# Points in the selection of experts weigh about 1.37 times as much when picks are handed out

## What is computed

```python
q = (xc @ w_q).reshape(t, PEER_HEADS, 2, PEER_QDIM // 2)
sc = jnp.einsum('thpc,hpnc->thpn', q, sub_keys)
v_half, i_half = lax.top_k(sc, PEER_TOPK_HALF)                 # 16 lists of 128 scores, 16 kept of each
cand = (v_half[:, :, 0, :, None] + v_half[:, :, 1, None, :]).reshape(t, PEER_HEADS, -1)
cand_idx = (i_half[:, :, 0, :, None] * PEER_NKEYS + i_half[:, :, 1, None, :]).reshape(t, PEER_HEADS, -1)
top_s, pos = lax.top_k(cand, PEER_TOPK)
expert = jnp.take_along_axis(cand_idx, pos, axis=-1)
g = jax.nn.softmax(top_s, axis=-1)
u = u_tab[expert]
act = jax.nn.gelu(jnp.einsum('thkd,td->thk', u, xc), approximate=False)
return jnp.einsum('thk,thkd->td', g * act, v_tab[expert])
```

## Time and profile before

| | us |
|---|---|
| median of 3 runs | 2128.93 |
| lowest and highest | 2127.93, 2129.14 |
| the profiled execution | 2127.96 |
| its span, first to last instruction | 2126.2 |
| affected feeds, first gathered row to third expert list | about 180 to 1286 |
| fourth feed, to its last row | to 1665 |

### The profile page before, as it was taken

How to read it: one execution, slowest core, us unless ns; L and a number is a source line. 1 busy time by engine, 2 the same in 40 slices (tenths; PEclk the granted TensorE clock), 3 DMA queues, 4 the chain that set the end, 5 groups by cost and what they waited for, 6 DMA issues and landing times.

```text
span 2126.2 us, 20672 instructions
## 1 busy us (share of the span) xinstructions
PE 1665.4 (78%) x6490; PEld 1005.3 (47%) x6490; DVE 1490.8 (70%) x3129; ACT 785.7 (37%) x2050; POOL 643.3 (30%) x524
## 2 busy tenths in 40 slices
PE   8797777667777865887778478765767899999998
PEld 4473343622323453333344433554333465668986
DVE  5378876897756688976666897668787465566654
ACT  1213452234424422432452235212555343454432
POOL 0013444335433343643344354425444000000000
PEclk9999989879898987989889799987888999999999
DMA  7358999999999999999999999999999785574452
GB/s 274 148 213 365 421 399 421 419 421 422 418 421 401 416 421 411 413 420 421 416 373 421 412 389 421 421 421 422 400 412 392 308 306 202 194 281 160 178 178 99
DMA packets 105803, 746.87 MB, mean 351 GB/s; under 512 B 12896, under 2 KB 13536, under 8 KB 16608
## 3 DMA queue, kind: packets, MB, share of 16 engines
q0 software_dynamic: 73728, 536.90, 61.4%
q1 hardware_dynamic: 31536, 207.08, 25.1%
q10 hardware_dynamic: 432, 1.57, 0.2%
HBM read 744.46 MB, written 1.05 MB: 351 GB/s over the span
## 4 chain that ended last, share of the span: by engine, by line
PE 39%; DMA 23%; DVE 20%; ACT 10%; issue 6%; DVEq 1%; PEldq 1%; PEld 0%; ACTq 0%; SPq 0%; POOL 0%; POOLq 0%
DMA sb_work<-in_peer_uv,sb_expert 17%; PE ps_acc L1570 11%; PE bank L496 5%; DVE sb_work L1534 5%; PE bank L1363 4%; DVE sb_x L1542 3%; DMA sb_ninth<-in_peer_uv,sb_expert 3%; PE bank L2060 2%; DMA sb_wring<-in_peer_w_q 2%; ACT L1550 2%; PE bank L777 2%; PE bank L566 2%; PE ps_acc L566 2%; PE ps_acc L568 2%; PE ps_acc L567 2%
## 5 line engine op out<-in xcount | busy, mean ns | idle before, releaser
L2694 POOL DMA_INDIRECT sb_work<-in_peer_uv,sb_expert x456 | 567.8, 1245 | 916.8 <-PE ps_acc L1570 401.8
L1570 PE MATMUL ps_acc<-sb_work,sb_diag 128*128 128x512 f32 x1184 | 626.9, 676 | 255.3 <-ACT sb_diag L1559 218.2
L1534 DVE CUSTOM_DVE_ANT_0 sb_work<-sb_work,sb_h 128x1024 f32<-128x1024 f32 x456 | 551.0, 1222 | 147.9 <-DMA sb_work<-in_peer_uv,sb_expert 138.7
L1570 PEld LDWEIGHTS ps_acc<-sb_work,sb_diag 128*128 128x128 f32 x1184 | 242.9, 216 | 586.2 <-issue 577.1
L1550 ACT ACTIVATE sb_dots<-sb_dots 128x1 f32<-128x1 f32 x512 | 102.1, 199 | 501.8 <-DVE sb_dots L1534 471.2
L1542 DVE SCALAR_TENSOR_TENSOR sb_x<-sb_work,sb_weight,sb_x 128x1024 f32<-128x1024 f32 x160 | 205.0, 1281 | 72.3 <-ACT sb_weight L1551 72.3
L560 DVE TENSOR_TENSOR sb_work_r<-sb_wring,sb_work_r 128x2048 fp32r<-128x2048 f32 (+1 forms) x74 | 133.8, 1828 | 101.0 <-ACT sb_work_r L553 100.4
L1551 ACT ACTIVATE sb_weight<-sb_dots,sb_share 128x1 f32<-128x1 f32 x512 | 150.8, 294 | 16.6
L553 ACT CAST sb_work_r<-sb_wring 128x2048 fp32r<-128x2048 f32 (+1 forms) x74 | 111.8, 1536 | 108.8 <-PE ps_acc L568 39.1
L1363 PE MATMUL bank<-sb_hT,sb_wring 128*128 128x128 f32 x1024 | 125.0, 287 | 24.3 <-DMA sb_wring<-in_peer_w_q 21.8
L1363 PEld LDWEIGHTS bank<-sb_hT,sb_wring 128*128 128x128 f32 x1024 | 123.2, 203 | 27.7 <-issue 26.6
(11 more groups left out here) (362 smaller groups left out, 2391.1 us busy)
## 6 DMA issues: line engine op xcount, KB each, us to landing
sb_wring<-in_w_mix SPq DMA_DIRECT2D x36, 1024.0 KB
sb_wring<-in_peer_w_q SPq DMA_DIRECT2D x32, 1024.0 KB
sb_wring<-in_w_gate SPq DMA_DIRECT2D x32, 1024.0 KB
sb_wring<-in_w_up SPq DMA_DIRECT2D x16, 1024.0 KB
sb_wring<-in_w_down SPq DMA_DIRECT2D x16, 1024.0 KB
sb_wring<-in_mla_w_uq SPq DMA_DIRECT2D x12, 768.0 KB
sb_work<-in_hyb_w_in SPq DMA_DIRECT2D x8, 1024.0 KB, 14.7
sb_wring<-in_hyb_w_out SPq DMA_DIRECT2D x8, 1024.0 KB
```

Of the source, the lines that this page charges most:

```text
L1534: e.tensor_tensor_reduce(u, u, h[:, t, :], 1.0, 0.0, ALU.mult, ALU.add, dots[:, i:i + 1]).then_inc(dot_ready, 1)
L1570: last = e.matmul(ps_acc[:, b * 512:(b + 1) * 512], diag[:, number % DIAGS, :], row(n)[:, D + b * 512:D + (b + 1) * 512], start=k == f["fi ...
L2694: pool.indirect_dma_start(row(n), None, a["peer_uv"], bass.IndirectOffsetOnAxis(ap=expert[:, t, n % P:n % P + 1], axis=0)).then_inc(row_la ...
```

## The change

```diff
@@ -1340,7 +1340,7 @@
             made = [point(7.0, "pe") for _ in range(4)] + [point(7.0, "pe")]
-            ranked = [point(us) for us in [6.0] + 5 * [3.5] + [6.0] + 6 * [4.5]]
+            ranked = [point(us) for us in [8.0] + 5 * [5.0] + [8.0] + 6 * [6.0]]
```

## The result

The changed kernel takes 2149.66 us in the median (2146.2 to 2150.87), the one before 2129.03 beside it (2127.93 to 2130.85): a ratio of 1.0093, 95% interval 1.0079 to 1.0107. I forecast 2131 with a range of 2124 to 2138. The kernel is 20.6 us slower, and the prediction was wrong.

The account below looks back on a forecast made before the run. The prediction took DMA to pace the three affected feeds. Selects -1.5, list work 0, attentions +3.7 and other stages 0 summed to +2.2 us on the profiled 2127.96, about 2131 us as a median; range 2124 to 2138.

Parts of the forecast that it names:

- The DMA paces the feeds: From 200 to 1286 us: 413 of 421 GB/s, so only 20.6 us of unused DMA time can alter.
- DVE waits for landing rows in the selects: Sign of being right: the ring nearly runs dry, and DVE shows waits in the selects that it didn't have before.
- the gap at the select's start: Selects: 8 us between two gather issues, expected to stay because the select's first dot doesn't move.
- the term of -1.5 us: Selects: denser picks fill faster what follows the starting gap; bounds -5.8 us and 0.
- (a): Selects: denser picks close the starting gap, 5.8 us come back and attentions lose nothing, 2123 us; chance 0.12.
- (c): End of the selects: the expert list comes late and DMA idles; 5 us a feed would be 2144; chance 0.05.
- The attention's term, +3.7 us: Attentions: two picks fewer each, 1.75 us given back of 2.49 us per pick; bounds -0.5 and +8.0 us.
- eleven additions pass from DVE to PE: Adder's side: PE's share of the moved work is hidden behind DMA, given no time in the sum.
- Rival (b): Attentions run short of requests, 8.0 us lost, 2136 us; sign: an attention under 370 GB/s; chance 0.23.
- The list work's term, 0 to +0.6 us: List work ahead of the select: each pick costs DVE 2.34 us and frees 2.49 us of DMA; taken as 0.
- "All other stages", 0 to +1 us: Norms, turns and projections: 3 or 4 picks per feed leave, running at 420 and 421 GB/s; taken as 0.
- DVE's 63.1 us: Last select with 32 dots: DVE's time for it, 26.3 + 36.8 us, against 55.1 us with 25 dots.

Follow-up runs that it names:

- with the pattern held: DVE adds the last pick of each attention point instead of every third by number: 2120.57 us with the old weights, 2132.10 us with the changed ones.
- the attention alone: Kernel before with only the attention's picks lowered (23, 20, 20 for 25, 22, 22): 2129.49 us; with DVE adding each point's last pick, 2120.92 us.
- the list work alone: Kernel before with only the list work's picks lowered (17, 14, 14 for 18, 16, 16): 2138.03 us; with DVE adding each attention point's last pick, 2123.78 us.
- The dense select alone: Kernel before with only the select's picks raised (36, 32, 32 for 29, 25, 25): 2139.08 us; with DVE adding each attention point's last pick, 2126.42 us.
- DVE last: Changed kernel, but DVE adds the last pick of each attention point instead of every third by number: 2132.10 us, 0.9995 to 1.0026 of the kernel before.
- the dense select alone with the old adders: Kernel before with only the select's picks raised (36, 32, 32), DVE still adding every third pick by number: 2139.08 us, ratio 1.0036 to 1.0068.
- the kernel with attention and list work low: Kernel before with attention (23, 20, 20 picks) and list work (17, 14, 14) lowered, select as before: 2137.71 us, ratio 1.0028 to 1.0057.

## Why the prediction was wrong

**What held.** The DMA paces the feeds: all of the loss is unused DMA time. DVE waits for landing rows in the selects, as forecast, where it didn't before (the last select of the changed kernel):

```profile
DVE sb_work L1534 <- DMA sb_work<-in_peer_uv,sb_expert: 6.9, 10, 1.9
```

and the gap at the select's start stays, with 1238.31 - 1230.41 = 7.9 us between two issues of GpSimd (8.0 before):

```profile
1230.41 0.94 POOL L2694 DMA_INDIRECT sb_work<-in_peer_uv,sb_expert  x1 [1.53 <-PE ps_acc L1570]
1238.31 1.15 POOL L2694 DMA_INDIRECT sb_work<-in_peer_uv,sb_expert  x1 [6.96 <-PE ps_acc L1570]
```

The selects' rate went to 397 and 399 GB/s from 404 and 395, and their unused time from 6 to 8 us, so nothing came back and the term of -1.5 us was 0 or above. Rivals (a) and (c) did not happen.

**The attention's term, +3.7 us, was wrong in its mechanism.** I asked what a pick less gives back and took 1.75 us from the chain's additions; with the pattern held it was 2.3 us, and the attention alone costs 0.4 us. But the step that failed is another one: I saw in the order of instructions that the additions "shift by one point", I counted that "eleven additions pass from DVE to PE", called this "hidden behind DMA", and gave it no price. Which pick of a point DVE adds is worth 9 us of this change: the unused time of the three attentions goes from 13 to 21 us with it and from 8 to 7 without it. Its rows were in the trace of before: PE's 7.72 us for three picks in the chain is such a piece (2.51 us of wait for a diagonal stand ahead of it), and ACT's wait for L763 stood in its list of waits with 41.7 us in the three feeds. Rival (b) had the right place and its sign came (357 GB/s in the third attention, under 370), and even its price of 8 us is what the attentions lost in unused time. That is luck: it came from the adders and not from picks that give back too little.

**The list work's term, 0 to +0.6 us, was mis-sized.** I priced a pick there from one quarter (1208.26 to 1220.62), which DVE paces, and applied 2.34 us to all five points. The picks that went in feeds 2 and 3 were at the first and third point, and around them DVE waits for ACT, ACT for PE and PE for the load of `w_q`: the first one gives back nothing in the 20.05 us ahead of the first MAX. The traces have 7 to 8 us more unused there; by the medians the list work alone costs 3.2 us with the pattern held, and that size isn't settled.

**"All other stages", 0 to +1 us, and the select.** I had 3 to 4 picks per feed from stages that run at 420 GB/s, giving back all of their DMA time. The dense select alone takes 7 picks per feed from them and costs 5.9 us with the pattern held. In the changed kernel the other stages have 6 us unused for 1, and 3.9 of them lie between the third attention and its ranking (3.2 with DVE last, 0.0 before), for which I had 0. The select itself lasts 70 to 84 us, as in the changed kernel. I had put DVE's 63.1 us beside a DMA-paced end without saying which of them would rule; it was the DMA (DVE is busy 63.0 of 71 us). That changes nothing in the sum by itself, since seven rows must pass somewhere. In the dense select alone the loss sits ahead: between 205 us and the first attention 4.0 us are unused (0.1 without the dense select), and in the third attention 8.5 (4.8 without it). The first stands also in the dense select alone with the old adders (3.4) but not in the changed kernel (0.0), so this is a place, not yet a cause; which stage there runs out of picks to hand out stays open. Two slips of the working change nothing: rival (a) has 55.4 us for the select's 55.1, and 0.2% around 2131 is 2127 to 2135, not 2126 to 2133.

## What to carry to other kernels

Where background work is dealt out by weight, changing one weight re-deals everything behind it: look at which piece of work lands first and last at each point, and which engine does it, before counting how many. What a piece of work less gives back must be read at the very place that loses it; one quarter of a stage can be paced by an engine and the quarter ahead of it by a weight load. If an order by number (every third pick) happens to fit, tie it to the place instead: give the newest item to the engine on which nothing waits.

## What the runs showed of the hardware

The costs kept their size in the changed kernel: dots of 1.15, additions of 1.19 on DVE, and rows at 421 GB/s where nothing else holds them up. What I had not expected is how sensitive ACT is when its program serves two streams: the copies for the attention and for the ranking share it with the weights of the picks, and moving only which of three picks PE adds changed one wait of ACT from 40.1 to 7.1 us in 129 us of the program. GpSimd's gather issue took 0.94 us at its shortest; in the kernel before all six issues of 3.0 us or more started within 0.1 us behind a two-input product of DVE over 2048 columns (L1482 or L1485). In all kernels that were timed for the experiments the executions of one kernel spread by 5 to 14 us, and a trace is one of them: the kernel with attention and list work low was profiled at 2127.99 us and has a median of 2137.71.
